# Filling unit cut at the layer boundaries, weight copy ahead of the row scaling, inverse root in two operations

## The reference, cut to what matters

```python
def rmsnorm(x, g):
    xf = x.astype(jnp.float32)
    y = xf * lax.rsqrt(jnp.mean(xf * xf, axis=-1, keepdims=True) + EPS)
    return (y * g.astype(jnp.float32)).astype(x.dtype)
...
        x = x + mixed
        hn = rmsnorm(x, ffn_norm[layer])
        x = x + (jax.nn.silu(hn @ ffn_w_gate[layer]) * (hn @ ffn_w_up[layer])) @ ffn_w_down[layer]
...
        x = x + memory_cross_attention(h, m, cross_wq[l], cross_wk[l], cross_wv[l], cross_wo[l])
```

## Time and profile before

| | before |
|---|---|
| median of three runs | 1284.28 us |
| profiled execution, its own time | 1293.12 us |
| its span (first to last instruction) | 1291.3 us |
| TensorE busy | 1217.2 us, 94% |
| VectorE busy | 790.2 us, 61% |
| ScalarE busy | 596.3 us, 46% |
| GpSimd busy | 72.5 us, 6% |
| read from HBM | 203.04 MB, 158 GB/s over the span |
| mean granted clock of TensorE | 0.966 of full speed |

### The profile page before, as it was taken

The page is one execution under the profiler, slowest core; times in us unless marked ns, Lnnn a source line. Parts: engine busy times, 40 slices in busy tenths (PEclk is TensorE's granted clock), DMA queues, the critical chain, the costliest instruction groups (busy, mean ns, idle before and its releaser), DMA issues.

```text
span 1291.3 us, 17676 instructions
## 1 busy us (share of the span) xinstructions
PE 1217.2 (94%) x7057; PEld 1049.6 (81%) x7057; DVE 790.2 (61%) x849; ACT 596.3 (46%) x732; POOL 72.5 (6%) x118
## 2 busy tenths in 40 slices
PE   6967899999999999999999999999979988999997
PEld 5855788888899988888888888887769877888886
DVE  6875666666654446666667666666574544666665
ACT  5444653443465655443445434445454544443443
POOL 2010100000002210000000000000011101000000
PEclk8886999999999999999999999999988999999999
DMA  8242445665543446555665556554422543456661
GB/s 211 67 105 96 136 149 193 195 191 183 179 163 131 131 131 196 194 180 182 193 195 161 180 182 193 194 185 153 152 99 98 164 130 113 148 182 193 195 191 69
DMA packets 157222, 206.04 MB, mean 160 GB/s; under 512 B 8936, under 2 KB 130352, under 8 KB 157168
## 3 DMA queue, kind: packets, MB, share of 16 engines
q1 hardware_dynamic: 157168, 205.28, 50.0%
HBM read 203.04 MB, written 1.05 MB: 158 GB/s over the span
## 4 chain that ended last, share of the span: by engine, by line
PE 84%; DVE 7%; ACT 5%; POOL 2%; issue 2%; DMA 1%; SPq 0%; POOLq 0%; ACTq 0%; DVEq 0%
PE outp L722 26%; PE acc L663 18%; PE outp L663 17%; PE outp L724 13%; DVE w_lo L1820 2%; ACT w_hi L1383 2%; PE acc L769 2%; PE outp L692 2%; PE outp L680 1%; DMA raw<-in_even_w_in_dram 1%; DVE arena L1965 1%; ACT xn L1392 1%; POOL arena L1316 1%; PE acc L1243 1%; PE acc L1263 1%
## 5 line engine op out<-in xcount | busy, mean ns | idle before, releaser
L1383 ACT ACTIVATE w_hi<-raw 128x2048 fp32r<-128x2048 f32 x183 | 351.1, 1919 | 466.2 <-PE outp L724 301.4
L1820 DVE TENSOR_TENSOR w_lo<-raw,w_hi 128x2048 fp32r<-128x2048 f32 x183 | 419.2, 2291 | 233.0 <-ACT w_hi L1383 233.0
L722 PE MATMUL outp<-h_pair,w_hi 128*128 128x512 f32 x1408 | 503.0, 401 | 3.3 <-DVE h_pair L1857 3.3
L724 PE MATMUL outp<-h_pair,w_lo 128*128 128x256 f32 x1408 | 397.0, 282 | 0.0
L722 PEld LDWEIGHTS outp<-h_pair,w_hi 128*128 128x128 f32 x1408 | 266.6, 189 | 70.4 <-DVE w_lo L1820 2.3
L724 PEld LDWEIGHTS outp<-h_pair,w_lo 128*128 128x128 f32 x1408 | 268.0, 190 | 1.4
L663 PE MATMUL outp<-w_hi,h_pair 128*128 128x512 f32 (+1 forms) x544 | 156.7, 374 | 2.6 <-DVE w_lo L1820 1.5
L663 PE MATMUL acc<-w_hi,f_hi 128*128 128x512 f32 x352 | 138.2, 393 | 0.0
L663 PE MATMUL acc<-w_lo,f_hi 128*128 128x512 f32 x352 | 137.6, 391 | 0.0
L663 PE MATMUL acc<-w_hi,f_lo 128*128 128x512 f32 x352 | 137.2, 390 | 0.0
L663 PEld LDWEIGHTS outp<-w_hi,h_pair 128*128 128x128 f32 x544 | 99.0, 193 | 21.5 <-DVE w_lo L1820 3.6
(11 more groups left out here) (278 smaller groups left out, 1189.4 us busy)
## 6 DMA issues: line engine op xcount, KB each, us to landing
raw<-in_ffn_w_gate_dram SPq DMA_DIRECT2D x44, 1024.0 KB, 5.6
raw<-in_ffn_w_up_dram SPq DMA_DIRECT2D x44, 1024.0 KB, 5.6
raw<-in_ffn_w_down_dram SPq DMA_DIRECT2D x44, 1024.0 KB, 4.9
raw<-in_odd_w_in_dram SPq DMA_DIRECT2D x12, 1024.0 KB, 5.2
raw<-in_w_in_dram SPq DMA_DIRECT2D x10, 1024.0 KB, 5.3
raw<-in_even_w_in_dram SPq DMA_DIRECT2D x5, 1024.0 KB, 9.2
raw<-in_even_w_out_dram SPq DMA_DIRECT2D x4, 1024.0 KB, 7.5
raw<-in_cross_wk_dram SPq DMA_DIRECT2D x4, 1024.0 KB, 5.8
```

The lines of the kernel that those rows point to most:

```text
L722: nc.tensor.matmul(bank.rearrange("p (a l) -> p a l", l=L), wh, h_pair[:, :, c, :], start=c == 0, stop=c == C - 1, skip_group_check=True)
L724: ins = nc.tensor.matmul(bank[:, 0:L], wl, h_hi[:, c, :], start=False, stop=c == C - 1, skip_group_check=True)
L1383: A(w_hi[:, u % 2, :], raw[:, u % RAW, :], ACT.Copy).then_inc(w_hi_ready, 1)
L1820: tt(w_lo[:, u % 2, :], raw[:, u % RAW, :], w_hi[:, u % 2, :].bitcast(F32), ALU.subtract).then_inc(w_lo_ready, 1)
```

## The change

Three edits. First, at the five boundaries with a filling unit TensorE runs its first half, the flips of t=0, the first half of the second half (chunks 0 to 3, a quarter of the unit, 12 matmuls), the flips of t=1, and the last quarter. Second, ScalarE's `norm` runs `split(u)` between `squares` and `norm_rows` instead of behind it (norms 2, 3, 4, 5 and 7; the others pass no unit there). Third, the sums of squares come already divided by 1024 (the square's scale is 1024 to the power -0.5, in VectorE's the factor 1/1024), and GpSimd makes the inverse root for every norm but 6 with two operations per row tile: one that adds the second sum, given as a scalar operand from SBUF, and EPS; and the power. It waits for both sums before the first of them.

```diff
-            def proj_t(u, k, fresh=None, x=(h_hi, h_lo), halves=(0, 1)):
+            def proj_t(u, k, fresh=None, x=(h_hi, h_lo), halves=(0, 1), cs=range(C)):
...
-                    for c in range(C):
+                    for c in cs:
...
-                if 1 in halves:
+                if 1 in halves and C - 1 in cs:
                     ins.then_inc(w_used, 1)
...
+            def mem_part(name, half, cs):
+
+                (proj_t if MEM_UNITS[name][0] == "k" else proj_n)(UNITS[name], OUT[name], x=(m_hi, m_lo),
+                                                                  halves=(half,), cs=cs)
...
-            def norm(n):
+            def norm(n, mem=None):
 
                 k = ACC[f"norm{n}"]
+                if mem:
+                    mem_half(mem, 0)
                 for t in range(T):
+                    if mem and t == 1:
+                        mem_part(mem, 1, range(4))
                     pe.wait_ge(xn_v, 2 * NTH[n] + 1 + t)
...
+                if mem:
+                    mem_part(mem, 1, range(4, C))
...
-                mem_half("mem_k0", 0)
-                norm(2)
-                mem_half("mem_k0", 1)
+                norm(2, "mem_k0")
...
-                        elif h == 0:
-                            own.link(gp.tensor_scalar(r, q, 1 / D, EPS, ALU.mult, ALU.add))
-                            first = r
-                        else:
-                            own.link(gp.tensor_scalar(r, q, 1 / D, None, ALU.mult))
-                            own.link(gp.tensor_tensor(first, first, r, ALU.add))
-                            gp.tensor_tensor(first, first, half[:, 0:1], ALU.pow).then_inc(rms_ready, 1)
+                    if n != 6:
+                        r = rms[:, i, 2 * t:2 * t + 1]
+                        own.link(gp.tensor_scalar(r, ss[:, i, 2 * t:2 * t + 1], ss[:, i, 2 * t + 1:2 * t + 2], EPS,
+                                                  ALU.add, ALU.add))
+                        gp.tensor_tensor(r, r, half[:, 0:1], ALU.pow).then_inc(rms_ready, 1)
...
-                    A(xn[:, t, c], src[:, t, c], ACT.Square,
+                    A(xn[:, t, c], src[:, t, c], ACT.Square, scale=1.0 if n == 6 else D ** -0.5,
...
                 squares(n, src)
-                norm_rows(n, src)
                 if u is not None:
                     split(u)
+                norm_rows(n, src)
                 norm_parts(n, gain)
```

More of the change, by code:

```diff
@@ L695, in whole_n @@
                     ins.then_inc(w_used, 1)
-            def proj_t(u, k, fresh=None, x=(h_hi, h_lo), halves=(0, 1)):
+            def proj_t(u, k, fresh=None, x=(h_hi, h_lo), halves=(0, 1), cs=range(C)):
                 w = w_unit(u, UW)
-                if 0 in halves:
+                if 0 in halves and 0 in cs:
                     out_taken(pe, k)
                 for m in halves:
-                    for c in range(C):
+                    for c in cs:
                         if fresh and m == 0 and c % 2 == 0:
@@ L726, in proj_both, with proj_n @@
                 ins.then_inc(w_used, 1)
-            def proj_n(u, k, fresh=None, x=(h_hi, h_lo), halves=(0, 1)):
+            def proj_n(u, k, fresh=None, x=(h_hi, h_lo), halves=(0, 1), cs=range(C)):
                 w = w_unit(u, UW)
                 for t in halves:
-                    if t == 0:
+                    if t == 0 and 0 in cs:
                         out_taken(pe, k)
-                    for c in range(C):
+                    for c in cs:
                         if fresh and t == 0 and c % 2 == 0:
@@ L796, in ffn @@
                 u0, k0, d0 = UNITS[name], OUT[name], ACC[name]
[L797 to L801, removed]
+                norm(n, mem)
                 proj_both(u0, k0, fresh=chunks(n))
@@ L1156, in mix @@
                 u0, k0 = UNITS["mix"], OUT["mix"]
-                mem_half("mem_v0", 0)
-                norm(5)
-                mem_half("mem_v0", 1)
+                norm(5, "mem_v0")
                 def q_of(b, h):
@@ L1228, in cross @@
                 u0 = UNITS["cross"]
-                mem_half("mem_v3", 0)
-                norm(7)
-                mem_half("mem_v3", 1)
+                norm(7, "mem_v3")
                 for j in range(4):
@@ L1298, in norm @@
                 i = NTH[n]
+                pieces = [p for p in x_order(n) if p[0] == 1 or n not in (0, 8)]
                 for t in range(T):
@@ L1303, in norm @@
                         else:
-                            at = [p for p in x_order(n) if p[0] == 1 or n not in (0, 8)].index((t, h))
-                            pool.wait_ge(sq_a, SQ_A[n] + at + 1)
-                        r, q = [v[:, i, 2 * t + h:2 * t + h + 1] for v in (rms, ss)]
+                            pool.wait_ge(sq_a, SQ_A[n] + pieces.index((t, h)) + 1)
                         if n == 6:
+                            r, q = [v[:, i, 2 * t + h:2 * t + h + 1] for v in (rms, ss)]
                             own.link(gp.tensor_scalar(r, q, 2 / D, EPS, ALU.mult, ALU.add))
                             gp.tensor_tensor(r, r, half[:, 0:1], ALU.pow).then_inc(rms_ready, 1)
-                        elif h == 0:
-                            own.link(gp.tensor_scalar(r, q, 1 / D, EPS, ALU.mult, ALU.add))
-                            first = r
-                        else:
-                            own.link(gp.tensor_scalar(r, q, 1 / D, None, ALU.mult))
-                            own.link(gp.tensor_tensor(first, first, r, ALU.add))
-                            gp.tensor_tensor(first, first, half[:, 0:1], ALU.pow).then_inc(rms_ready, 1)
+                    if n != 6:
[3 more added lines that the diff above has]
+                        gp.tensor_tensor(r, r, half[:, 0:1], ALU.pow).then_inc(rms_ready, 1)
             def root(x, n, scale, eps, done):
@@ L1827, in norm_front @@
                         c = slice(h * 512, (h + 1) * 512)
-                        V.tensor_tensor_reduce(out=xn[:, 0, c], in0=src[:, 0, c], in1=src[:, 0, c], scale=1.0,
+                        V.tensor_tensor_reduce(out=xn[:, 0, c], in0=src[:, 0, c], in1=src[:, 0, c], scale=1 / D,
                                                scalar=0.0, op0=ALU.mult, op1=ALU.add,
```

3 lines of the change are left out of this document (1 added, 2 removed).

## The result

The changed kernel takes 1279.4 us (median of 6 runs, 1276.7 to 1282.4) where the kernel before, in 6 runs of its own, takes 1288.7 (1283.5 to 1293.1): ratio 0.9932, interval 0.9908 to 0.9956. It is faster by 0.7%, which is clear of the scatter, but by less than forecast: 9.3 us and not 13.1. The time lies above the upper end of the stated range, 1278. The profiled execution took 1279.77, span 1277.9.

A forecast was written before the change was run, and what follows sets the result against it. TensorE holds 84% of the chain of waits, so time is won where it stands still, at the norms. Terms 2.7 + 2.1 + 2.7 + 2.1 + 2.1 + 0.85 + 0.3 + 0.27 = 13.1; 1284.3 - 13.1 = 1271.2 us, range 1266.5 to 1278.

The forecast's parts named there:

- The boundaries: Norms 2, 3, 4, 5 and 7, with a filling unit: gains of 2.7, 2.1, 2.7, 2.1 and 2.1 us.
- The signs set down: Changed profile: no bracket at t=1's flips, copy behind squares, first product 7.65 us (norms 2, 4) or 7.6 (3, 7) after filling.
- The pace: Layer's first product behind a filled norm: lag behind VectorE's h_lo falls to at most 0.1, giving 0.15 us more.
- norm 9: No filling unit; TensorE waits for t=1's flips, which the earlier root brings forward: 0.85 us gained.
- The path: Filled norms: ScalarE copies weights before multiplying gains, VectorE's h_lo follows, and TensorE's first product gets the last of these.
- The root: GpSimd's root: new first operation taken as 0.22 us; t=0 ready 0.3 earlier, t=1 0.88 earlier at norm 2.
- Rival 2: Second units' weights come late at all five boundaries, giving back 4 to 5 us: 1276; chance 0.16.
- Rival 1: TensorE's clock stays up at norms 1 and 9, 3 us lost at each before: 1265, or 1268 if one; chance 0.12.
- Rival 3: GpSimd's new operation with an SBUF operand is slow: gain gone at 1.16 us, 1290 to 1294 at 2.17; chance 0.04.

The follow-up runs named there:

- the slow root: The kernel after, with three repeated one-column GpSimd adds, to no purpose, ahead of each root: 1286.9 us, one run.
- filled holes: Matmuls and transposes nobody reads put in TensorE's holes at norms 1 and 9: 1284.2 us on the kernel before, 1271.2 on the kernel after.

## Why the prediction was right and wrong

**The boundaries: the lengths right, each to 0.2 us.** The signs set down hold at norms 2 to 5 and 7: no bracket at the flips of t=1, the copy behind the squares, gains 0.43 behind the flips (0.45 said), the length 7.73 (7.65 said) and 7.48 (7.6 said). The gain is 11.6, less the 0.5 lost in the mixer 11.1, where 2.7 + 2.1 + 2.7 + 2.1 + 2.1 = 11.7 was forecast (the fourth, norm 5's 2.1, already with 0.4 lost in the mixer).

**The pace: put at 0.15 a boundary, worth nothing.** The forecast's 11.7 holds 0.15 at norms 2, 3, 4 and 7 for a product that lags less behind VectorE, 0.6 in all. The rows show none of it: 24 matmuls of the product take 3.07 us at norm 2 where they took 3.08, since VectorE has the first quarter of `h_lo` ready at 352.5, only just before TensorE asks for it at 352.75. This term is 0.6 of the 0.8 by which the sum was too large; norm 9 is another 0.2, and every other term is within 0.1. The pace was there to be had with copy and root alone (2.88).

**The path.** The copy alone and the quarters alone show that the path named was the one that held: VectorE's `h_lo` behind ScalarE's gains behind the copy.

**The root: right in kind, its new operation too cheap.** It takes 0.30 and not 0.22, and 0.67 when VectorE's scaling of 1024 columns runs beside it. The same instruction is 0.67 at 347.45, beside L1842 from 347.20 to 347.95, and 0.30 with VectorE idle; in the slow root it is 0.30 at both row tiles. The Trainium skill, GPSIMD Engine Reference, section 1 (Specifications), says that the two engines share SBUF interfaces, with contention in a two-port mode of VectorE or with two SBUF inputs. These rows agree as far as they go; that L1842 ran in such a mode no row shows. So norm 9 gave 0.6 instead of 0.85.

**Rival 2, the weights.** The new wait is at the one place named, 0.34 on TensorE and 0.49 in all; at the other four boundaries there is none.

**Rival 1, the clock: not what happened, and too dear as told.** Norm 9 stayed at the lower level (0.59). So did norm 1 (0.60, as before). But in the second profile of the same kernel the window that lies 2.76 behind the first flip of norm 1 shows the upper level,

```profile
154.61:162.61 8.00, 6.74 (x39) 5.59 (x39) 5.75 (x10) 4.79 (x10) 0.00 (x0) 1.00 0.38 130
```

and the FFN behind it took 184.9, as with filled holes, instead of 186.5: the level there differs between executions of one kernel. Its worth is 1.8 to 2.0 at each place, where "3 us lost at each" stood. Those 3 us counted all of the low stretch as work that runs at half speed. But in the same window TensorE is busy 7.35 us at 0.60 and 6.74 at 1.00: at the upper level it stands and waits for part of what the lower level costs. That this is all of the difference isn't shown.

**Rival 3's price** doesn't follow from its own formula: at 2.17 us the operation is 1.95 over 0.22, and 16 x 1.95 less the 2 of slack is 29 us on top of 1271, some 1300 and not 1290 to 1294. No run went there.

**The step that failed** is the last one: "... the holes are spans of waiting on fixed instruction lengths and should be as large in both. 1284.3 - 13.1 = 1271.2 us." The holes at the filled boundaries are as large in every profile, to 0.02 us. The 1284.3 isn't the kernel's level. In the 47 runs of the kernel before that ran beside the experiments the median is 1287.95, so the median of the three that were there at first lay 3.7 low, and that it stood 8.8 under the profiled execution was a sign of it. Beside the result itself the kernel before had 1288.7: of the 8.2 us by which 1279.4 misses 1271.2, 4.4 are this base, and the other 3.8 are a gain of 9.3 where 13.1 was forecast. Over 12 runs, the six of the result and six more, the kernel after has 1277.97. The account over all runs:

```
forecast                                            1271.2
base: median of 47 runs, not of three               +3.7
the sum was 12.3 in the trace, not 13.1             +0.8
remainder                                           +2.3
measured, median of 12 runs                         1278.0
```

The remainder goes with the clock. In the runs of all kernels together the time rises with the share of the span that ran at the lower clock, by 0.63 us for each us of (1 - mean granted clock) x span. The kernel before has a mean of 0.9726, after 0.9703; the product is 2.7 us larger after, and that gives 1.7. Compared at an equal clock the change is worth 11.75, give or take 1.0 (two standard errors), which agrees with the trace's 12.3. Whether the tighter kernel gets a lower clock by itself or these twelve runs had it by chance is open; the difference of the two clocks is two of its standard errors, nearly all of it lies in the first six runs, and where in the span it would fall no single profile pair can say.

So the path through the engines was right, and more than half of the miss (3.7 of 6.8) was the number it was taken from; the pace term, the rest of the sum's excess and the clock make up what is left. Against the right base the forecast gain of 13.1 stands beside 10.0 measured (1287.95 less 1277.97) and 12.3 traced.

## What to carry to other kernels

Take out the latest link before feeding the engine that waits for it: the same reordering of matmuls was worth nothing alone and some 2.6 us once the copy and root were out of the way. Before a change of 1% is forecast in absolute time, ask how far the base is known: three runs of a kernel that scatters by 10 us fix it to some 4 us, and the profile's stretches at the boundaries, which repeat to 0.02 us, carry the difference far better than the total does. A hole in TensorE's work can cost a second time behind itself, by the lower clock (here 1.8 to 2.0 us), and matmuls that nothing reads can be worth their place.

## What the hardware showed that I had not expected

The granted clock differs between executions of the same kernel (mean 0.966 to 0.978 in 47 runs of the kernel before) with no difference in the instructions, and the scatter goes with it: the line of 0.63 us above takes up about two thirds of its variance in those 47 runs. The FFNs away from holes repeat to within 0.7 us in all profiles, while the first block, the mixer and the stretches behind norms 1 and 9 differ by up to 6 us. Filling the two holes raised the mean clock to 0.977 to 0.978 in the three kernels that had it.

One-column operations of GpSimd cost by their kind: 0.19 for an add of two tensors, 0.22 for a multiply and add with immediates, 0.30 with one scalar from SBUF, 0.56 for the power; and 0.67 for the third while VectorE scales 1024 columns.
